# Routing and experts of a mixture-of-experts layer: the branch on the part count placed ahead of selection and token split, expert outputs scaled per slot and spread in two rounded passes

## The reference

```
def _moe_ffn(h, router, w1, w3, w2):
    logits = (xt @ router).astype(jnp.float32)
    top_logit, top_idx = lax.top_k(logits, TOP_K)      # 2 of 8 experts
    gates = jax.nn.softmax(top_logit, axis=-1)
    ...
        yb = _swiglu(xb, w1[e], w3[e], w2[e])          # (silu(x@w1[e]) * (x@w3[e])) @ w2[e]
    ...
    out = jax.ops.segment_sum(y_s * weight_s[:, None], token_s, num_segments=T)
```

## Time and profile before

| | us |
|---|---|
| median of three timed runs | 1641.64 |
| profiled execution, its own time | 1633.31 |
| its span, first to last instruction | 1631.5 |
| routing, from the first logits matmul to the first gather matmul | 878.46 to 902.20 |
| gather, to the first expert matmul | 902.20 to 917.76 |
| experts 0 to 7 | 917.76 to 1321.8 |

### The profile page before, as it was taken

How to read it: one execution, slowest core, us unless ns; L and a number is a source line. 1 busy time by engine, 2 the same in 40 slices (tenths; PEclk the granted TensorE clock), 3 DMA queues, 4 the chain that set the end, 5 groups by cost and what they waited for, 6 DMA issues and landing times. The chain is left out here.

```text
span 1631.5 us, 24583 instructions
## 1 busy us (share of the span) xinstructions
PE 1546.8 (95%) x9902; PEld 1339.9 (82%) x9902; DVE 1119.5 (69%) x1642; ACT 810.5 (50%) x1083; POOL 18.4 (1%) x21
## 2 busy tenths in 40 slices
PE   8899989999999989998997899999999999978998
PEld 7789979899999978987986677777777779966677
DVE  5778864756555677886475788888888875257534
ACT  4643435354444464343533677777776744353422
POOL 1000000000000000000001000000000000000000
PEclk9999999999999999999999899999999998889999
DMA  8332222345556443222243399999999974412121
GB/s 315 132 127 91 91 91 91 122 163 183 192 181 194 161 143 117 91 91 91 91 156 121 126 342 351 345 339 335 346 358 340 341 260 159 139 65 78 65 92 64
DMA packets 82051, 292.95 MB, mean 180 GB/s; under 512 B 9095, under 2 KB 11647, under 8 KB 81679
## 3 DMA queue, kind: packets, MB, share of 16 engines
q1 hardware_dynamic: 81935, 291.34, 50.8%
HBM read 290.22 MB, written 1.08 MB: 179 GB/s over the span
## 5 line engine op out<-in xcount | busy, mean ns | idle before, releaser
L377 DVE TENSOR_TENSOR ring_lo<-ring,weights_hi 128x1024 fp32r<-128x1024 f32 x343 | 413.6, 1222 | 240.7 <-ACT weights_hi L356 238.0
L356 ACT ACTIVATE weights_hi<-ring 128x1024 fp32r<-128x1024 f32 x343 | 355.8, 1056 | 194.9 <-PE bank_P L272 158.4
L270 PE MATMUL bank_P<-h_hi,weights_hi 128*128 128x256 f32 x1456 | 427.9, 294 | 14.1 <-DVE ring_lo L377 8.5
L272 PE MATMUL bank_P<-h_hi,ring_lo 128*128 128x256 f32 x1456 | 414.6, 285 | 0.0
L271 PE MATMUL bank_P<-h_lo,weights_hi 128*128 128x256 f32 x1456 | 413.6, 284 | 0.0
L270 PEld LDWEIGHTS bank_P<-h_hi,weights_hi 128*128 128x128 f32 x1456 | 278.9, 192 | 24.7 <-issue 6.7
L272 PEld LDWEIGHTS bank_P<-h_hi,ring_lo 128*128 128x128 f32 x1456 | 283.0, 194 | 0.0
L271 PEld LDWEIGHTS bank_P<-h_lo,weights_hi 128*128 128x128 f32 x1456 | 279.1, 192 | 1.2 <-issue 0.5
L271 PE MATMUL bank_P<-ring_lo,gathered_hi 128*96 128x512 f32 (+1 forms) x384 | 144.0, 375 | 0.0
L377 DVE TENSOR_TENSOR ring_lo<-ring,tokens_hi 128x1024 fp32r<-128x1024 f32 x76 | 90.4, 1217 | 2.3 <-ACT tokens_hi L356 2.3
L377 DVE TENSOR_TENSOR ring_lo<-ring,tokens_lo 128x1024 fp32r<-128x1024 f32 x74 | 88.2, 1216 | 2.3 <-ACT tokens_lo L356 2.3
(11 more groups left out here) (501 smaller groups left out, 2718.5 us busy)
## 6 DMA issues: line engine op xcount, KB each, us to landing
ring<-stream SPq DMA_DIRECT2D x541, 512.0 KB, 4.5
cst<-consts SPq DMA_DIRECT2D x1, 1712.0 KB, 10.8
arena<-params SPq DMA_DIRECT2D x1, 1211.0 KB, 6.7
arena<-x SPq DMA_DIRECT2D x1, 1024.0 KB, 5.1
arena<-bias_vec SPq DMA_DIRECT2D x8, 128.0 KB, 2.9
out<-arena SPq DMA_DIRECT2D x2, 512.0 KB, 2.6
arena<-params SPq DMA_DIRECT2D x2, 256.0 KB, 7.7
arena<-bias_vec SPq DMA_DIRECT2D x8, 64.0 KB, 2.8
```

What stands on the lines that cost most here:

```text
L270: pe.matmul(out, hi, x_hi, start=start, stop=False, skip_group_check=True)
L272: return pe.matmul(out, lo, x_hi, start=False, stop=stop, skip_group_check=True)
L356: a.activation(self.slots[i % len(self.slots)], env["ring"][:, slot, :], ACT.Copy)\
L377: v.tensor_tensor(env["ring_lo"][:, slot, :], env["ring"][:, slot, :], self.slots[i % len(self.slots)].bitcast(F32), ALU.subtract).then_in ...
```

## The change

The diff, cut to its core:

```diff
-    selw = cut(EXPERTS, TT2, CAP)
-    back = cut(EXPERTS, T)
+    back = rounded(env, cut, "slots_to_tokens", EXPERTS, T)
...
-    gather_banks = (P0, P1, Z0, Z1, BO, BC, BY, BX)
+    gather_banks = (Z0, Z1, BO, BY, P0, P1, BC, BX)
...
-        sp.wait_ge(*after("vec"))
-        sp.wait_ge(*after("vec_end"))
-        sp.dma_start(env["dram"]["bias_vec"].rearrange("(i h) n -> h i n", i=2), vec[0:8, :, 0:512])\
-          .then_inc(env["sem"]("vec_stored"), 16)
         sp.wait_ge(*after("parts"))
...
-                mm = pe.matmul(Z1[0:8, 0:T], rg[:, k, :], x[:, k, :], start=(k == 0), stop=(k == KD - 1))
-                if k == 0:
-                    env["mix1_blocks"].release(mm)
+                for a in range(TT2):
+                    mm = pe.matmul(Z1[:, a * 8:(a + 1) * 8], x[:, k, a * P:(a + 1) * P], rg[:, k, :], start=(k + a == 0),
+                                   stop=(k == KD - 1), skip_group_check=True)
+                    if k + a == 0:
+                        env["mix1_blocks"].release(mm)
             if q == 3:
-                mm.then_inc(*done("pe", "logitsT"))
+                mm.then_inc(*done("pe", "logits"))
...
         for q in range(4):
             pe.wait_ge(*after(f"x_{q}", "mix1"))
             logits(q)
+        for q in range(4):
             turn(q)
-        pe.wait_ge(*after("lgT"))
-        for a in range(TT2):
-            mm = pe.transpose(Z1[:, T + a * 8:T + a * 8 + 8], lgT[0:8, a * P:(a + 1) * P], ident[0:8, 0:8])
-        mm.then_inc(*done("pe", "logits"))
...
         pe.matmul(Z0[:, 16:24], C("ones"), chosen[:, 1, :], start=False, stop=True).then_inc(*done("pe", "ranks"))
+        pe.wait_ge(env["sem"]("params2_in"), 16)
+        bias_vectors(pe).then_inc(*done("pe", "p_vec"))
...
     def routing_scalar(a):
+        env["expert_hi_parts"] = HiParts(env, a, MOE_AT, range(EXPERTS * EXP_BLOCKS), "moe", slots=slots)
+        env["expert_hi_parts"].upto(len(env["w_hi"]))
+        a.activation(dm_exp, eps("norm").broadcast_to([P, 2]), ACT.Sqrt).then_inc(*done("act"))
...
-        a.wait_ge(*after("token_rms"))
-        for half in range(2):
-            for t in range(TT2):
-                a.activation(htm[0][:, t, half * 512:(half + 1) * 512], tm_bank(t, half), ACT.Identity, scale=rt[:, t:t + 1])\
-                 .then_inc(*done("act", f"htm_hi_{half}_{t}"))
...
-        v.wait_ge(*after("logitsT"))
-        link(v.tensor_copy(lgT[0:8, :], Z1[0:8, 0:T]), "lgT")
+        env["expert_lo_parts"] = LoParts(env, v, MOE_AT, range(EXPERTS * EXP_BLOCKS), "moe", slots=slots)
+        env["expert_lo_parts"].upto(1)
...
         tt(chosen, oh1, oh2, ADD, "chosen")
-        v.wait_ge(*after("token_root"))
+        env["expert_lo_parts"].upto(2)
+        v.wait_ge(*after("squares_1_1"))
+        tt(ss[:, 0, :], ss[:, 0, :], ss[:, 1, :], ADD, "token_squares")
         tt(dm, m2[:, :, 0], m1[:, :, 0], SUB)
-        tt(dm, dm, rt, MUL, "gate_diff")
-
...
         link(v.tensor_copy(parts, most[:, 1:2]), "parts")
-        slot_numbers = C("iota").unsqueeze(1).broadcast_to([P, EXPERTS, CAP])
-        for a in range(TT2):
-            tt(sel[:, :, a, :], slot_numbers, rank[:, a, :].unsqueeze(2).broadcast_to([P, EXPERTS, CAP]), ALU.is_equal,
-               "sel" if a else None)
-        low_parts(1)
+        v.wait_ge(*after("token_root"))
+        link(v.reciprocal(rt, rt), "token_rms")
+        tt(dm, dm, rt, MUL, "gate_diff")
...
     def sync(sp):
+        sp.wait_ge(*after("vec"))
+        sp.wait_ge(*after("vec_end", "routing"))
+        sp.dma_start(env["dram"]["bias_vec"].rearrange("(i h) n -> h i n", i=2), vec[0:8, :, 0:512])\
+          .then_inc(env["sem"]("vec_stored", "routing"), 16)
         load_blocks(env, sp, MOE_AT + RING, SEC_AT + RING)
...
     def tensor(pe):
-        pe.wait_ge(*after("htm_lo_1_1", "routing"))
+        pe.wait_ge(*after("rank", "routing"))
         for n in range(2 * KD):
             g, k = n // KD, n % KD
+            if n in (0, 4):
+                pe.wait_ge(*after(f"htm_lo_{n // 4}_1"))
+            if n == 4:
+                pe.wait_ge(*after("vec"))
             if n >= 8:
                 pe.wait_ge(*after(f"hE_lo_{n - 8}"))
...
         def scatter(e):
 
-            pe.wait_ge(*after(f"y_{e}"))
             for q in range(4):
+                if q % 2 == 0:
+                    pe.wait_ge(*after(f"y_lo_{e}_{q // 2}"))
                 for j in range(2):
                     k = 2 * q + j
-                    mm = pe.matmul(x_banks[q][:, j * T:(j + 1) * T], ysb[0:CAP, k * P:(k + 1) * P], back[0:CAP, e, :],
-                                   start=(e == 0 and j == 0), stop=(e == EXPERTS - 1 and j == 1), skip_group_check=True)
+                    for y in (y_hi, y_lo):
+                        mm = pe.matmul(x_banks[q][:, j * T:(j + 1) * T], y[0:CAP, k * P:(k + 1) * P], back[0:CAP, e, :],
+                                       start=(e == 0 and j == 0 and y is y_hi),
+                                       stop=(e == EXPERTS - 1 and j == 1 and y is y_lo), skip_group_check=True)
                 if e == EXPERTS - 1:
...
+            pe.wait_ge(*after("hE_lo_14"))
...
-        pe.wait_ge(*after("hE_lo_15"))
+        def weights():
+
+            pe.wait_ge(*after("hE_lo_15"))
+            pe.wait_ge(*after("w8"))
+            for e in range(EXPERTS):
+                for a in range(TT2):
+                    mm = pe.matmul(BX[0:CAP, e:e + 1], sel[:, e, a, :].bitcast(F32), w8[:, a, e:e + 1], start=(a == 0),
+                                   stop=(a == 1))
+            mm.then_inc(*done("pe", "p_slot_weight"))
+
+        pe.wait_ge(*after("hE_lo_12"))
         for e in range(EXPERTS):
             group(e, 0, 0, 4)
             if e == 0:
                 backs()
+                weights()
+                pe.wait_ge(*after("hE_lo_13"))
...
             group(e, 1, 2, 4)
+            if e == 0:
+                pe.wait_ge(*after("slot_weight"))
...
+        a.wait_ge(*after("token_rms", "routing"))
+        for half in range(2):
+            for t in range(TT2):
+                a.activation(htm[0][:, t, half * 512:(half + 1) * 512], tm_bank(t, half), ACT.Identity, scale=rt[:, t:t + 1])\
+                 .then_inc(*done("act", f"htm_hi_{half}_{t}"))
...
+        a.wait_ge(*after("gate_diff", "routing"))
+        a.activation(dm_exp, dm, ACT.Exp).then_inc(*done("act", "gate_exp"))
...
-                a.activation(ysb[0:CAP, half * 512:(half + 1) * 512], bank[0:CAP, :], ACT.Copy)\
-                 .then_inc(*(done("act", f"y_{e}") if half else done("act")))
+                a.activation(y_hi[0:CAP, half * 512:(half + 1) * 512], bank[0:CAP, :], ACT.Identity,
+                             scale=slot_weight[0:CAP, e:e + 1]).then_inc(*done("act", f"y_hi_{e}_{half}"))
...
-            if n == 12:
-                lo.upto(2)
...
-        for a in range(TT2):
-            tt(selw[:, :, a, :], sel[:, :, a, :].bitcast(F32), w8[:, a, :].unsqueeze(2).broadcast_to([P, EXPERTS, CAP]), MUL,
-               "selw" if a else None)
...
+                if e == 0 and n == 5:
+                    v.wait_ge(*after("p_slot_weight"))
+                    link(v.tensor_copy(slot_weight[0:CAP, :], BX[0:CAP, 0:EXPERTS]), "slot_weight")
...
-            lo.upto((e + 1) * EXP_BLOCKS + 2)
+            lo.upto((e + 1) * EXP_BLOCKS + BLOCK_LEAD)
+            for half, bank in enumerate((BY, BX)):
+                c = slice(half * 512, (half + 1) * 512)
+                v.wait_ge(*after(f"y_hi_{e}_{half}"))
+                v.scalar_tensor_tensor(out=y_lo[0:CAP, c], in0=bank[0:CAP, :], scalar=slot_weight[0:CAP, e:e + 1],
+                                       in1=y_hi[0:CAP, c].bitcast(F32), op0=MUL, op1=SUB).then_inc(*done("dve", f"y_lo_{e}_{half}"))
```

More of the change, by code:

```diff
@@ L1470, in gathered_sections @@
                       for part in ("hi", "lo"))
-    ysb = cut(D)
+    y_hi, y_lo = (rounded(env, cut, f"expert_output_{part}", 1, D)[:, 0, :] for part in ("hi", "lo"))
     vec = cut(2, 768)
     assert cut.at[0] <= PARAMS2_AT, cut.at[0]
-    squares = ysb[:, 0:512]
+    squares = sl.rearrange("p a n -> p (a n)")
+    env.update(gate_diff=dm, gate_exp=dm_exp, gates=g12, first=oh1, second=oh2, second_weights=over, rank=rank, tm_bank=None)
     cut.at[0] = PARAMS2_AT
@@ L1479, in gathered_sections @@
     tm_bank = lambda a, half: (BO, BC, BY, BX)[2 * a + half]
-    gather_banks = (P0, P1, Z0, Z1, BO, BC, BY, BX)
+    env["tm_bank"] = tm_bank
+    gather_banks = (Z0, Z1, BO, BY, P0, P1, BC, BX)
     BLOCK_LEAD = 3
@@ L1732, in scalar @@
     def scalar(a):
-        hi = HiParts(env, a, MOE_AT, range(EXPERTS * EXP_BLOCKS), slots=slots)
-        hi.upto(2)
+        hi = env["expert_hi_parts"]
+        a.wait_ge(*after("token_rms", "routing"))
[3 more added lines that the diff above has]
+                 .then_inc(*done("act", f"htm_hi_{half}_{t}"))
+        a.wait_ge(*after("p_vec", "routing"))
+        for i in range(2):
```

(11 more changed lines are left out.)

97 lines of the change are left out of this document (58 added, 39 removed).

## The result

The changed kernel took 1617.53 us in the median of 4 runs (1614.97 to 1619.23), the kernel before 1641.58 us (4 runs, 1639.8 to 1641.85): ratio 0.986, 95% interval 0.983 to 0.989. The forecast was 1626.3 us with 1621 to 1635 as its range: the direction was right, the size too small. Later pairs with more runs gave 0.9894 (0.9867 to 0.9921, 6 runs against 23) and 0.9894 (0.9873 to 0.9916, 6 against 11), that is about 17.4 us less.

A forecast was written before the change was run, and what follows sets the result against it. PE was taken to bound the experts, and the last engine at the barrier the routing. Terms -6.5 - 1.5 + 3.6 - 10.9 = -15.3 us, from the median 1641.64, gave 1626.3 us; range 1621 to 1635.

The forecast's parts named there:

- the last step of the sum: Whole kernel: carried -15.3 us from the profiled execution (1618.0) onto the timed median 1641.64, giving 1626.3 us.
- Rival 1: Experts: DMA becomes the bound and the scatter saving may be lost entirely, total -4.4 us, 1637.2 us; chance 0.12.
- Part 1: Routing up to the barrier: it opens at 890.9 instead of 897.43, bias vector last at half clock; -6.5 us.
- Rival 4: Routing: the clock holds until the branch, bias vector takes 1.88 us, barrier opens at 889.0; 1624.4 us; chance 0.20.
- Part 2: From barrier to experts: gather 0.1 us later behind the barrier, wait before first expert nearly gone (-1.6); together -1.5 us.
- Rival 2: Behind the branch: DVE comes late, its code starting as late as PE's, up to 2.4 us; 1628.7 us; chance 0.08.
- Part 3: Expert 0: slot weights add 32 one-column matmul instructions on PE; +3.6 us, bounds 2.8 and 5.5.
- Part 4: Scatter: 16 rounded passes take 1.9 instead of 3.45 us, saving 1.55 each in seven experts; -10.9 us.
- Rival 3: Expert boundaries: y_lo holds up DVE's lo parts, PE loses 3.3 us at each of 7, +23.1; 1649.4 us; chance 0.04.

The follow-up runs named there:

- first repeat: The changed kernel, unchanged, run again and timed against 23 runs of the kernel before: 1620.63 us (6 runs, 1616.39 to 1627.14).
- second repeat: The changed kernel, unchanged, run once more as the scale for three other kernels on one chip: 1620.22 us (6 runs, 1615.09 to 1620.70).

## Why the prediction was right or wrong, point by point

- **Wrong: the last step of the sum.** "The median of the timed runs lies 8.3 us above that execution; the prediction is for the median: 1641.64 - 15.3." It treated the 8.3 us as something that every run of either kernel carries. The runs showed in its place a gap that changes from execution to execution: 51 later runs of the kernel before take 1632.28 to 1642.95 us, by how many stretches at 1.2 GHz fall into unchanged code ahead of the routing. The three runs known at the time, 1641.52 to 1641.85, all lay near its upper end. The changed kernel spreads as widely, 1615 to 1627, and its first four runs lay near the lower end. The miss of 8.8 us has three parts: the first median of the kernel before is 3.4 us above the 1638.17 of its later runs, that of the changed kernel 3.1 us below the 1620.63 of its first repeat, and the change is worth 17.5 us between these, 2.2 more than the sum (16.1 by stages, 0.8 more). Rival 1 guessed at memory as the reason for the 8.3 us. In the traces the clock is the reason. One thing stays open: only 11 of the 51 later runs took 1639.8 us or more, as all four of the first session did, so runs of one session seem to share something, and nothing here shows what.
- **Part 1, right in mechanism.** The bias vector was last at the barrier and at half clock; without it DVE is last. The end at 890.86, forecast 890.9, is luck and hides two errors: the logits started 2.2 us earlier, and from them to the barrier it took 14.6 us, not 12.4, because the clock fell under the logits already and the ranks ran at half clock as well (0.43 us from one to the next instead of 0.23), the bound the text named. The gain at the gather's start was 4.3 us in this execution, 5.9 and 7.2 in the two repeats, where the logits had 2.4 GHz; forecast 6.5.
- **Rival 4** (the clock holds until the branch) didn't happen in any execution of the changed kernel. The nearest was the second repeat, where the bias vector took 3.19 us. The rule of the Trainium skill ("TensorE: Matmul & The Clock Gate", "Why this matters for your kernels") that was cited for it ties drops in mid-kernel to idle gaps between bursts. The trace disagrees: PE was busy for 8.30 of the 8.30 us ahead of the logits and under all of them, and the clock fell in their midst.
- **Part 2, right in mechanism, too small at first.** Gather start 4.80 us behind the barrier (forecast 4.87), ACT and DVE back after 0.96 and 1.13, no wait before the first expert. From gather to experts it took 12.9, 13.0 and 14.0 us instead of 15.6, a gain of 1.5 to 2.7 against 1.5. Both parts together gave 7.0, 8.4 and 8.7; forecast 8.0. Rival 2 didn't occur.
- **Part 3: +3.6 forecast, 4.0 measured, of other make.** To the first turned hidden tile it took 14.3 instead of 10.25 us. The weights' own matmuls take 2.7, nearer to the lower bound (2.8, scaled to their 96 loaded columns); they also stream one column instead of eight, and no run separates the two. The rest is the stretch at 1.2 GHz behind them, which no part had: without it, in the second repeat, the same distance was 12.8 us, 2.5 more than before.
- **Part 4, right, slightly small.** The 16 passes stand 0.12 us apart. An expert became 1.65 us shorter, 1.55 forecast; over seven -11.6, not -10.9. Half of the change alone shows the same, and one pass less shortens an expert by 0.95 more. Rival 3 has nothing for it: y_lo shows up in no wait before the eighth scatter, where PE waits 1.44 us for it; there DVE's lo parts hid it, and x came 0.2 us later behind the last expert.
- **Rival 1 (DMA)** fell: 357 GB/s, and 362 with one pass, with PE busy throughout.
- **The stage behind the x add** was +1.6 us in the first pair. Over all executions it is 306.7 to 309.5 before and 307.9 to 309.1 after: spread, not the change.

## What to carry to other kernels

A sum built from one profiled execution predicts another profiled execution. Before it is carried onto a median, ask whether the gap between the two is a constant or a draw: the granted clock of each run tells (here 0.969 at 1641 us, 0.976 at 1633), and a gap that changes from run to run belongs into the range at both ends. Judge an edit worth 2 us by the stage it stands in, over two or three profiles; medians of 12 and 23 runs of the same kernel lay 3.2 us apart here. And where all engines meet at a branch, take what nobody needs soon out of the way of the last to arrive, for PE came back 4.6 to 5.1 us behind it whenever nothing else held it.

## What the runs showed of the hardware that was not expected

- The same program at the same place got 2.4 GHz in one execution and 1.2 in the next. Of eight executions of the two kernels, those with the logits at 876 to 879 us had 6.8 to 10.2 us at 1.2 GHz ahead of them, those at 881 to 885 had 17.1 to 23.9. One such stretch of 3.4 us cost 1.2 to 1.7 us in the slowest of them.
- Behind the barrier with its branch PE started after 4.57 to 5.07 us in six executions with the old routing, and after 4.95 us with the bias vector behind the branch, with nothing to wait for in any of them. DVE and ACT started after 0.94 to 1.35 us where they had nothing to wait for.
- Behind 16 transposes and 32 one-column instructions without any idle time the clock fell to 1.2 GHz for 3.4 us in two of three executions of the changed kernel, at 2.4 GHz before and after. Of the nine executions of all kernels with this piece of code six had it.
